# A decoder step on one core: the rows of the dilated-cache copies dealt to the DMA engines in strided order

## What is computed

```python
def reference(...):
    # modulation from c: shift, scale, gate for both halves of the layer
    hs = rms_norm(xs, norm_mix[layer]) * (1.0 + sc1_s) + sh1_s
    qa_s, ka_s, va_s, qb_s, kb_s, vb_s = project_qkv(hs, w_in[layer], pos_s)
    past_k = cache_sb_k[layer][page_table]...          # paged keys and values, 16 pages a sample
    oa_s = stick_breaking(qa_s, k_all, v_all, pos_s, bias_l)
    ext_k = jnp.concatenate([cache_dil_k[layer], kb_s], axis=1)
    ext_v = jnp.concatenate([cache_dil_v[layer], vb_s], axis=1)
    ob_s = dilated_attention(qb_s, ext_k, ext_v, buf + jnp.arange(DEC_SEQ))
    xs = xs + g1_s * merge_out(oa_s, ob_s, norm_out_sb[layer], norm_out_dil[layer], w_out[layer])
    dk_s.append(ext_k[:, DEC_SEQ:]); dv_s.append(ext_v[:, DEC_SEQ:])
    # the same for the 256 prompt rows, without a past
    # then for all rows: q = h @ w_pq; top 16 of 16384 experts for 8 heads; u and v rows gathered
    fs = peer_ffn(hs2, w_peer_q[layer], peer_sub_keys[layer], peer_u[layer], peer_v[layer])
```

## Time and profile before

| | |
|---|---|
| median of three runs | 1355.5 us (1353.68, 1355.5, 1360.96) |
| profiled execution, its own time | 1358.96 us |
| its span | 1357.2 us |
| TensorE, VectorE busy | 1069.7 us (79%), 791.9 us (58%) |
| ScalarE, POOL busy | 375.4 us (28%), 390.9 us (29%) |
| packets of all queues | 91423, 479.79 MB |
| SP's queue (q1) | 44476 packets, 146.92 MB, 31.3% of 16 engines |
| POOL's queue (q0) | 46912 packets, 332.47 MB, 60.5% of 16 engines |

### The profile page before, as it was taken

How to read it: one execution, slowest core, us unless ns; L and a number is a source line. 1 busy time by engine, 2 the same in 40 slices (tenths; PEclk the granted TensorE clock), 3 DMA queues, 4 the chain that set the end, 5 groups by cost and what they waited for, 6 DMA issues and landing times.

```text
span 1357.2 us, 14727 instructions
## 1 busy us (share of the span) xinstructions
PE 1069.7 (79%) x3386; PEld 494.3 (36%) x3386; DVE 791.9 (58%) x1680; ACT 375.4 (28%) x1030; POOL 390.9 (29%) x384
## 2 busy tenths in 40 slices
PE   6899998888656657989997777877768777777775
PEld 2375774333211101558852323333323332332331
DVE  4203897887422411343437777776777677777756
ACT  1201004334110000012233333323344334444323
POOL 1000003020111000000135555554445545545541
PEclk9897999887677886988999999899899999999999
DMA  8999888899698887998669999999999999999995
GB/s 324 420 348 333 290 305 288 302 329 358 194 294 268 241 271 267 357 367 321 237 241 423 421 422 421 422 422 422 421 422 375 422 422 422 422 422 421 423 421 241
DMA packets 91423, 479.79 MB, mean 354 GB/s; under 512 B 11793, under 2 KB 11818, under 8 KB 50173
## 3 DMA queue, kind: packets, MB, share of 16 engines
q0 software_dynamic: 46912, 332.47, 60.5%
q1 hardware_dynamic: 44476, 146.92, 31.3%
HBM read 476.10 MB, written 70.32 MB: 403 GB/s over the span
## 4 chain that ended last, share of the span: by engine, by line
PE 35%; DMA 33%; issue 10%; DVE 8%; SPq 6%; ACT 4%; POOL 2%; POOLq 0%; DVEq 0%; ACTq 0%
DMA R<-in_uv,idst 24%; PE ps L513 13%; PE ps L798 8%; PE ps L751 4%; DMA R<-in_sb_k 3%; SPq L287 3%; DMA R<-in_sb_v 3%; SPq L288 2%; PE ps L475 2%; POOL R L435 2%; PE ps L602 2%; DVE R L1148 2%; DMA R<-out_dil_v_s 1%; DVE R L1462 1%; PE ps L484 1%
## 5 line engine op out<-in xcount | busy, mean ns | idle before, releaser
L798 PE MATMUL ps<-R,diag 128*128 128x512 f32 x1024 | 488.0, 626 | 147.5 <-ACT diag L1076 147.5
L435 POOL DMA_INDIRECT R<-in_uv,idst x256 | 322.0, 1258 | 331.4 <-PE ps L798 256.3
L1462 DVE CUSTOM_DVE_ANT_0 R<-R,H 128x1024 f32<-128x1024 f32 x264 | 318.7, 1223 | 162.3 <-DMA R<-in_uv,idst 151.9
L798 PEld LDWEIGHTS ps<-R,diag 128*128 128x128 f32 x1024 | 194.9, 198 | 440.5 <-ACT diag L1076 231.8
L513 PE MATMUL ps<-R,HT 128*128 128x256 f32 (+1 forms) x768 | 173.0, 385 | 1.0 <-DVE HT L1343 0.4
L381 POOL DMA_DIRECT2D R<-in_wts x44 | 23.5, 534 | 503.5 <-PE ps L513 329.3
L513 PEld LDWEIGHTS ps<-R,HT 128*128 128x128 f32 (+1 forms) x768 | 119.3, 159 | 55.5 <-issue 12.1
L602 PE MATMUL ps<-R,ast 128*32 128x512 f32 x256 | 80.5, 826 | 69.4 <-DMA R<-in_sb_v 65.9
L1054 ACT ACTIVATE gel<-dots 128x2 f32<-128x2 f32 x132 | 26.9, 204 | 376.4 <-DVE dots L1462 376.4
L1148 DVE TENSOR_TENSOR R<-R 128x1024 f32<-128x1024 f32 x64 | 78.3, 1223 | 72.7 <-ACT R L881 57.2
L475 PE MATMUL ps<-R,cT 128*9 128x256 f32 x384 | 96.8, 410 | 0.6 <-ACT bsel L828 0.6
(11 more groups left out here) (234 smaller groups left out, 858.2 us busy)
## 6 DMA issues: line engine op xcount, KB each, us to landing
R<-in_wts POOLq DMA_DIRECT2D x48, 1024.0 KB, 8.9
R<-in_sb_k SPq DMA_DIRECT2D x128, 256.0 KB, 4.7
R<-in_sb_v SPq DMA_DIRECT2D x128, 256.0 KB, 3.4
out_dil_k_s<-in_dil_k SPq DMA_DIRECT2D x32, 1023.5 KB, 8.3
out_dil_v_s<-in_dil_v SPq DMA_DIRECT2D x32, 1023.5 KB, 8.1
R<-in_uv,idst POOLq DMA_INDIRECT x256, 12.1
m_all<-in_dil_k POOLq DMA_DIRECT2D x16, 192.0 KB, 5.9
R<-in_dil_v SPq DMA_DIRECT2D x16, 192.0 KB
```

The source lines that it names most:

```text
L435: pool.indirect_dma_start(out=R[:, row_slot(k), :], out_offset=None, in_=A["uv"], in_offset=bass.IndirectOffsetOnAxis(ap=idst[:, par, k:k ...
L798: last = pe.matmul(ps[:, banks + q, :], diag[:, k % 4, :], R[:, row_slot(k), D + q * 512:D + (q + 1) * 512], start=False, stop=False, skip ...
L1462: dve.tensor_tensor_reduce(u, u, H[:, t, :], 1.0, 0.0, ALU.mult, ALU.add, dots[:, k:k + 1]).then_inc(s["dot_done"], 1)
```

## The change

Both sides of the copy are read in another order. Before, a piece is 128 rows one behind the other: `(r n)` with r = 128, n = 2,047, and the rows lie next to each other, so that the pattern is one run of memory, and each of the 16 DMA engines takes a sixteenth of it, 65,504 bytes. After, the piece is `(k r n)` with k = 8 and r = 16, walked as 16 rows by 8 by 2,047: the outer dimension has 16 entries, and entry r holds the rows r, r + 16, ..., r + 112. Each row is then a packet of 8,188 bytes. The bytes, the semaphores, the waits and the order on SP are the same.

```diff
                 landed = copied[2 * odd + m]
                 if not (isinstance(pair, int) and isinstance(q, int) and pair + q == 0):
                     sp.wait_ge(landed, pair * 64 + q * 16)
-                sp.dma_start(dst[bass.ds(pair * 2 + odd, 1), bass.ds(q * n, n)].rearrange("a (r n) -> (a r) n", r=P),
-                             src[bass.ds(pair * 2 + odd, 1), bass.ds(q * n + DG, n)].rearrange("a (r n) -> (a r) n", r=P)
+                sp.dma_start(dst[bass.ds(pair * 2 + odd, 1), bass.ds(q * n, n)].rearrange("a (k r n) -> (a r) k n", k=8, r=16),
+                             src[bass.ds(pair * 2 + odd, 1), bass.ds(q * n + DG, n)].rearrange("a (k r n) -> (a r) k n", k=8, r=16)
                              ).then_inc(landed, 16)
```

## The result

The changed kernel took 1384.67 us, the median of four runs (1382.52 to 1395.2), against 1356.12 us before (four runs, 1353.68 to 1360.96). The ratio is 1.0217, with a 95% interval of 1.0165 to 1.027: slower by 2.2%, where no change had been forecast. The interval lies clear of 1, but on both sides of 1.02. The profiled execution took 1395.2 us (span 1393.5 us) and is the longest of its kernel; before's took 1358.96 us. So what the two traces show adds up to 36 us, and about 28 of them are typical.

A forecast was written before the change was run, and what follows sets the result against it. No engine was taken as full, the chain being shared between TensorE and DMA. The terms summed to 0.2 + 0.2 = +0.4 us, against the median 1356 us, no change; the 8-in-10 range was 1349 to 1366 us.

The forecast's parts named there:

- Stage A: 31 to 127 us, 24 copy pieces beside TensorE's projection; to end 1.0 us later, inside 4.54 us of slack: 0.
- the idle time at 208 us: VectorE idles 4.54 us at 208.39 us, waiting for TensorE; taken as the slack of the copies from 31 to 127 us.
- the slower rival: Packet starts exposed: first price 3.09 us a piece, +8.4 us, 1364 us; worse end 1388 us; chance 0.20.
- term (1): What a piece costs the DMA engines: 2.75 us, 0.04 more than before, taken from the weights' 8 KB packets.
- The upper one that I computed, 3.81 us: Price of a piece were 8 KB to cost as four 2 KB packets: +33 us, 1388 us; chance 0.04.
- term (3): Who goes first where two queues meet: weights may land earlier, but TensorE never waits for them; 0.
- V and C: 318 to 510 us (10 pieces) and 520 to 551 us (6 pieces), with landings on the chain: +0.2 us each.
- The cover of stage D: 545 to 642 us, 24 pieces nothing on the chain waits for; ends 1.0 us later, 9 us before the gathers: 0.
- Term (2): SP's time to issue a piece, mostly 0.51 us; bounds -2.2 to +6.9 us on the path; taken as 0.
- Term (4): Pages behind a copy on SP's own queue: served in order, they stay behind the same bytes; 0.
- the faster rival: Transfers queued behind a copy gain from its being cut: -16.5 us, 1339 us; chance 0.11 with all partial forms.
- the likeliest case: Whole kernel unchanged within 0.5%: chance 0.69; alone it spans 1351 to 1362 us.

The follow-up runs named there:

- al8: The change's strided order with packets of 8,192 bytes, each starting on a 2 KB boundary: 1359.8 us, ratio 0.9987 to the kernel before.
- al64: The kernel before with 512-row pieces, one run of 65,536 bytes per engine, starting on 2 KB boundaries: 1358.53 us, ratio 0.9998.
- smallD: The kernel before with the change's packets only in the 24 copies after 545 us: 1359.37 us, ratio 0.9993.
- aftermv: The changed kernel with only 16 copies ahead of the fifth key chunk and 32 in the last group: 1384.56 us, ratio 1.0173 to the kernel before.
- gap8: The change's order and starts, but only the first 8,000 bytes of each row copied, so no shared lines: ratio 1.0084 to the kernel before.
- gapal: The change's order with 8,000-byte packets at aligned starts 8,192 bytes apart on both sides: ratio 1.0013 to the kernel before.
- rdmis: The change with destination rows aligned, 8,192 bytes apart, source rows still 8,188 bytes apart: 1369.03 us, ratio 1.0081 to the kernel before.
- mis64: The kernel before with one run of 65,500 bytes per engine, starting at 4-byte multiples: 1359.82 us, ratio 0.9996.
- wrmis: The change with source rows aligned, 8,192 bytes apart, destination rows still 8,188 bytes apart: 1402.24 us, ratio 1.0348 to the kernel before.

## Why the prediction was wrong

**Stages and mechanism.** The map of the kernel held. Stage A's copies had 4.54 us of slack and no more; the way from a dearer copy to the end (SP held, fifth chunk late, the idle time at 208 us used up) is that of the slower rival, and every step of it is in the trace. The gathers kept their stretch, 636.3 us for L798 against 634.8. Weights that land earlier were worth nothing.

**The step that failed is term (1), the price of a piece.** I took 2.75 us, "because it shares size, stretch and company" with the weights' packets; it is 3.45 us. The size did not matter (al8: 2.84 us at the same size). What the weights' row doesn't share is the destination: its rows go to SBUF, 8 KB to a partition, and of the copy's rows in HBM, 8,188 bytes apart, seven in eight start off a 32-byte boundary. That it is this and not HBM as such, al8 shows. The number 8,188 stood in the diff and in the text, and was used for one rule on transactions of 256 bytes only, where it made 0.08 us. No row of the trace before holds a small ragged write to HBM, so the bound had to come from the far rows. The upper one that I computed, 3.81 us, would have held it; I gave its neighbourhood a chance of 4%. One argument of term (3) failed with it: that stage A's end doesn't hang on the other queue, "the same bytes are through at 127 us". The bytes are the same, but the weights' packets became dearer too (0.343 to 0.415 us), so that SP was held for 26.2 us where 24 pieces at 0.74 us more make 17.8.

**The slower rival** had the right end and the wrong cause: a fixed start per packet was to cost 0.38 us a piece, and al8 against al64 leaves 0.07 us by the price and 0.2 by the last copy. Its formula, 34 x 0.74 - 4.5, would give 20.7 us, 1377 us. The 28.5 us measured (35.3 in the two traces, to the last gathered row) are more through stage A alone: there the formula has 24 x 0.74 - 4.5 = 13.3 us, and the traces 30.3. The difference is the 8.4 us by which the copies were held beyond their own price, the 6.7 us by which the page behind them took longer to land, and 1.5 us of further waits. For V and C it has too much, 3.0 and 4.4 us, where 1.5 and 1.8 came in.

**The cover of stage D** was right as far as it went: smallD's copies end 30 us later and cost nothing. aftermv shows its edge: with copies issued until 719 us, 19 us into the gathers' matmuls, they lose 20 us. In the change itself the last copy is issued at 698.5 us, 29 us ahead of them, since the whole kernel is later.

**Term (2)**, SP's time for an issue: 0.572 us in place of 0.510, over 13 pieces 0.8 us; taken as 0. **Term (4)**, the order within SP's queue, held: nothing queued behind a copy got through it earlier, and the faster rival had nothing.

The range ended at 1366 us, since the likeliest case and the first price of the slower rival were made to fill it. Both rested on the same belief, that the price of a packet is set by its length.

## What to carry to other kernels

Before a run of memory is cut into rows, look at where each piece starts in the destination: a row length that is not a multiple of 32 bytes makes most writes start off a boundary (seven in eight at 8,188 bytes, half at 8,176), and in these runs writes of 8 KB got dearer in the mean the more of them did, along with the other queue's packets. When a transfer that "only SP waits for" gets dearer, ask what is written behind it on SP's queue, how many us of idle time stand between that and the path, and where a stretch bound by DMA begins: moving the copies elsewhere only moves the bill once their room is full. When no row of the trace has the kind of transfer that a change makes, the far bound deserves a real chance.

## What the runs showed of the hardware

- An HBM-to-HBM copy in packets of 8 KB costs 0.01 us (by the price of a piece) to 0.03 us (by the last copy) for each packet more, if every packet starts on a 32-byte boundary (al8 against al64, 24 pieces of 8 packets per engine in place of 1).
- A packet of 8 KB whose destination starts off a 32-byte boundary costs about 0.06 us more in the mean by itself (gap8 against gapal, over all 192 packets per engine), and about 0.115 us where its neighbour ends in the same 32 bytes (the change against al8). These are figures of the last copy, and take in what the weights' queue lost; by the price of a piece they are 0.04 and 0.08 us. A ragged source or a ragged end costs little in stage A (rdmis), and a ragged start of a 64 KB packet nothing that can be seen (mis64).
- The cost isn't even: the median packet takes 0.309 us with aligned and with ragged starts, while those over 0.6 us go from 4.2% (al8) to 14.8% (the change), and the weights' packets on the same engines from a mean of 0.342 to 0.414 us.
- Off the boundary, interleaved rows end stage A 7.5 us later than rows in order (3.45 against 3.38 us a piece), with all lines shared between engines in the one and within an engine in the other.
- Not settled: what in the chip makes ragged starts dear, and why a ragged destination with an aligned source and shared lines (wrmis, 161.2 us) is dearer than the change, and what makes rdmis 0.8% slower as a whole.
